# A mixture-of-experts step on one Trainium2 core: token lists of experts 19 to 63 read from a DRAM table instead of built by matmuls, with the weight loads in another order

## The chip, the cores and the metric

The kernel runs on one core of one Trainium2 chip. The metric is the device time of one execution in microseconds (us); for each kernel the median over several executions is given. The profile is of one execution, and its span runs from the first to the last instruction.

## The reference, cut to what matters

384 tokens (128 context, 256 latent) of width 1024 pass through one layer: attention and a convolution branch, then a mixture of experts, all in fp32. The change is in the mixture of experts:

```python
scores = jax.nn.sigmoid((t @ router_w).astype(jnp.float32))
...
_, idx = lax.top_k(masked, TOP_K)                      # 8 of 64 experts for each token
w = jnp.take_along_axis(scores, idx, axis=-1)
w = w / jnp.sum(w, axis=-1, keepdims=True) * ROUTED_SCALE
gates = jnp.sum(jax.nn.one_hot(idx, N_EXPERTS, dtype=jnp.float32) * w[..., None], axis=1)
hid = jax.nn.silu(jnp.einsum('td,edf->tef', t, exp_w_gate)) * jnp.einsum('td,edf->tef', t, exp_w_up)
hid = hid * gates[:, :, None].astype(hid.dtype)
routed = jnp.einsum('tef,efd->td', hid, exp_w_down)    # 64 experts, hidden width 256
shared = (jax.nn.silu(t @ sh_w_gate) * (t @ sh_w_up)) @ sh_w_down
return (routed + shared).reshape(B, S, D)
```

## The kernel before, in words

The first part (attention, convolution, router) ends near 510 us, and then a loop over the 64 experts runs. An expert takes one **step** j. Its tokens, 48 on average, are laid in 128 slots; if some expert had more than 128 tokens, the steps would go round again, and register `last` is read from the routing for that. With this input there is one round: 64 steps, in blocks of UNROLL = 8. `in_order` writes out block 0 with constant step numbers, runs a `Fori` loop over blocks 1 to 6, and writes out the last block.

Each fp32 product is made of three fp32r matmuls (high x high, high x low, low x high, lines 1759 to 1761). So ACT makes the high half of each weight tile (`gate_up_hi` L1072, `down_hi` L1081), and DVE the low half (`gate_up_lo` L1463, `down_lo` L1592). One step on each engine, in the order of its queue:

- SP: three loads of 1 MB into `raw`. Each tile has two buffers, and a load waits until DVE has made the low half from what was in the buffer: gate of expert j+3, then up of j+3 (both in `load_gate_up`, L636, semaphore `glo_done`), then down of j+1 (`load_down`, L643, `dlo_done`).
- POOL: `gather` (L777) fetches the rows of the tokens of j+3 from `h2_d` by the indices in `ixt`; `scatter` (L786) writes the results of j-3 to `y_d`.
- PE: `token_list` for j+3 (L2085), `turn_tokens` for j+1 (8 transposes, L1769), `gate_up` for j (24 matmuls of 512 columns), `turn_hidden` for j-1 (2 transposes), `down` for j-2 (12 matmuls of 512 columns).
- DVE: `hidden` (j-1), `hidden_lo` (j-2), `gate_up_lo` (j+1, gate), `list_of` (j+3, L1564 and L1565), `onehot` (j+4, L1552), `turn_lo` (j+1), `down_lo` (j-1), `gate_up_lo` (j+1, up).
- ACT: `gate_act`, `hidden_hi`, `gate_up_hi` (gate), `rows_out`, `turn_hi`, `down_hi`, `gate_up_hi` (up).

The token list of an expert comes about so: DVE compares each token's slot number with the 128 slots (`onehot`, 128x384), PE multiplies these three 128x128 matrices by four values of each token (`token_list`, three matmuls of 4 columns), and DVE copies the sums into `ixt` (row to gather, row to write) and `gsl` (the gate weight).

After the loop, the eight results of each token are read back from `y_d` (`first_rows` L663 to L667 on SP within the last block, the others after it), added up with the shared expert and the residual, and normed with `fgr`, the last norm's weights. `fgr` is loaded by ACT's queue just before the loop (L1165).

Of the kernel before, what the change touches and what calls it, by code (L numbers as in the profile page):

```python
# [26 lines left out]
P = 128  # L27
D = 1024
KD = D // P
NT = 3  # L30
# [18 lines left out]
UNROLL = 8  # L49
NO_TOKEN = 4096  # L50
TAIL_SUMS = 4 * NT + 4


def constants():

    import numpy as np

    i = np.arange(P)
    parts = {"ident": np.eye(P), "before": (i[:, None] < i[None, :]), "ones": np.ones((P, P)),
             "slot": np.broadcast_to((i % 8 * 16 + i // 8)[None, :], (P, P))}  # L60
# [11 lines left out]
    parts["token"] = i[:, None] + P * np.arange(NT)[None, :]  # L72
    at, n = {}, 0
# [65 lines left out]
def hybrid_step(nc, x_prompt, x_sample, cache_ckv, cache_krope, c, c_ctx, mod_w, mod_b, norm1_g, w_in,  # L139
# [11 lines left out]
    with ExitStack() as ctx:  # L151
# [124 lines left out]
        token_i = sb("token_i", [P, 1], A + 5.9375, I32)  # L276
        gsl = sb("gsl", [P, UNROLL], R + 8.375)
        sg = sb("sg", [P, FF], R + 9)
        hd = [sb(f"hd{i}", [P, FF], R + 10 + i) for i in range(2)]
# [20 lines left out]
        mod_d = dram("mod_d", [2, 4 * D])  # L300
        y_d = dram("y_d", [T * TOPK, D])

        def conv_slot(k):
# [17 lines left out]
        sinv = cst_of("sin").rearrange("p (t a f) -> p t a f", t=2, a=2)  # L321
        token = cst_of("token")
        V_G1, V_CB, V_LG, V_LB, V_QG, V_C = 0, 8, 16, 24, 32, 35

# [18 lines left out]
        cks_out = sem("cks_out")  # L343
        zeros_done, sgc_done, z_done, conv_step = (sem(n) for n in ("zeros_done", "sgc_done", "z_done", "conv_step"))
        sgs_done, sgs_out = sem("sgs_done"), [sem(f"sgs_out{i}") for i in range(2)]
        qtok_done, qrope_done, qT_act, qT_dve = (sem(n) for n in ("qtok_done", "qrope_done", "qT_act", "qT_dve"))
# [11 lines left out]
        x1_done, h2_done = sem("x1_done"), sem("h2_done")  # L358
        x1_out = sem("x1_out")
        h2d_out = sem("h2d_out")  # L360
        h2g_done, h2T_done = sem("h2g_done"), sem("h2T_done")
# [37 lines left out]
        def read_by(g):  # L399
# [6 lines left out]
                "lat": lambda: (lat_done, NT * n + g[2] + 1),  # L406
                "ca": lambda: (z_done, n + 1), "cg": lambda: (sgc_done, n + 1),
                "qnT": lambda: (f_done, KD + n + 1), "ckT": lambda: (flo_done, KD + 3 + n + 1),
                "krT": lambda: (krT_done, 1), "gl": lambda: (sgs_done, n + 1),
                "uq": lambda: (qtok_done, NT * n + g[2] + 1), "uk": lambda: (kT_done, 2 * n + 2),  # L410
# [132 lines left out]
        def _(sp):  # L543
# [183 lines left out]
        def _(pool):  # L727
            pool.memset(zb[:, :, :], 0.0).then_inc(zeros_done, 1)

            pool.wait_ge(latn_done, 2 * NT)  # L730
# [50 lines left out]
            def scatter(i, k, last=False):  # L781
# [26 lines left out]
        def _(act):  # L808
# [89 lines left out]
            for j in range(KD):  # L898
                split(item_no[("conv", j)] + 2)
                p = got(act, ("cg", j))  # L900
                if j >= 2:
                    act.wait_ge(z_done, j - 1)
                act.activation(sgc[:, j % 2, :], p[:, 0:T], ACT.Sigmoid).then_inc(sgc_done, 1)
                if j == 1:
# [9 lines left out]
            def spill_gate(j):  # L914

                act.wait_ge(sgs_done, j + 1)
                act.dma_start(sig_d[j], sgs[:, j % 2, :]).then_inc(sgs_out[j % 2], 16)


            for j in range(16):  # L920
# [3 lines left out]
                if j >= 2:  # L924
                    act.wait_ge(sgs_out[j % 2], 16 * (j // 2))
                act.activation(sgs[:, j % 2, :], p[:, 0:T], ACT.Sigmoid).then_inc(sgs_done, 1)
                if j:
# [188 lines left out]
            def step(i, k, left=99):  # L1116
# [68 lines left out]
        def _(dve):  # L1185
# [120 lines left out]
            for j in range(KD):  # L1306
                split(item_no[("conv", j)] + 2)
                g = ("ca", j)
                p = got(dve, g)
                dve.wait_ge(sgc_done, j + 1)  # L1310
                for a, b, o in ((0, TC, PAD), (TC, T, 2 * PAD + TC)):
# [243 lines left out]
            def list_of(i, k):  # L1555
                j = i * UNROLL + k
                if isinstance(j, int) and j < 2:
                    p = got(dve, ("list", j))
                else:
# [42 lines left out]
            def hidden(i, k):  # L1602
                j = i * UNROLL + k
                dve.wait_ge(sg_done, j + 1)
                if from_step(j, 2):
# [3 lines left out]
                                         op0=ALU.mult, op1=ALU.mult).then_inc(hd_done, 1)  # L1609

            sums = {"all": 0}

# [29 lines left out]
            def step(i, k, left=99):  # L1642
# [31 lines left out]
            turn_lo(0, 0)  # L1674
            shared_hidden(2)
            in_order(dve, step)


# [64 lines left out]
        def _(pe):  # L1743
# [521 lines left out]
```

## Time and profile before

| | |
|---|---|
| median of 3 executions | 1181.88 us (1179.66 to 1182.85) |
| the profiled execution | 1178.6 us |
| its span | 1176.8 us, mean granted clock 0.990 |
| PE busy | 1126.8 us, 96% of the span |
| DVE / ACT / POOL busy | 88% / 68% / 20% |
| read from and written to HBM | 326.66 MB and 41.66 MB |

A row of a group of instructions has its line, engine, operation, tiles (out<-in, buffer numbers left out), shapes and count, then the busy time in us and the mean ns of one, then the engine's idle time just before them and what ended it. Matmuls overlap: the duration of one is about 0.39 us, while the next starts 0.23 us after it. So a busy PE is read from the distance of the starts.

### The profile page before, as it was taken

What the parts mean: (1) busy time and instruction counts of PE and PEld (TensorE: products, weight loads), DVE (VectorE), ACT (ScalarE), POOL (GpSimd) and SP (SyncE); (2) the same over time, 40 slices, a digit from 0 to 9 for tenths busy, and PEclk for the clock granted to TensorE, in tenths of its full rate; (3) what the DMA queues carried; (4) which work ended last, traced back from release to release, by engine and by line L of the source; (5) the groups of instructions that cost most, each with busy time, mean ns of one, the idle gap of its engine ahead of it and who ended that gap; (6) DMA issues with size and microseconds to landing.
All of it is one profiled execution on the core that took longest, in us unless ns stands there. A gap on an engine that the chain in (4) does not pass through costs nothing.

```text
span 1176.8 us, 16800 instructions
## 1 busy us (share of the span) xinstructions
PE 1126.8 (96%) x5641; PEld 919.4 (78%) x5641; DVE 1031.0 (88%) x1379; ACT 801.6 (68%) x996; POOL 238.9 (20%) x184
## 2 busy tenths in 40 slices
PE   4999999998998999989999999999999999999996
PEld 1699999864557898658888888888888888888862
DVE  4759999989997465779999999999999999999977
ACT  6553232777873642648888888888888888888842
POOL 1000000001114001122533223332323323232220
PEclk9999999998999989999999999999999999999998
DMA  9673456535547236868999999999999999999994
GB/s 347 189 184 107 135 155 171 170 130 160 164 142 212 77 106 240 331 243 319 384 372 375 371 379 366 381 363 347 356 349 359 353 363 372 364 372 371 357 412 201
DMA packets 123035, 328.06 MB, mean 279 GB/s; under 512 B 28280, under 2 KB 69847, under 8 KB 98151
## 3 DMA queue, kind: packets, MB, share of 16 engines
q1 hardware_dynamic: 98368, 289.34, 67.1%
q0 software_dynamic: 21648, 33.80, 8.5%
q10 hardware_dynamic: 2968, 4.26, 1.0%
q8 instruction: 30, 0.49, 0.2%
q14 instruction: 21, 0.17, 0.0%
HBM read 326.66 MB, written 41.66 MB: 313 GB/s over the span
## 4 chain that ended last, share of the span: by engine, by line
PE 82%; DVE 6%; ACT 5%; DMA 5%; issue 2%; SPq 0%; POOLq 0%; ACTq 0%; DVEq 0%
PE bank L1759 22%; PE bank L1761 22%; PE bank L1760 21%; PE bank L1769 8%; PE bank L1954 2%; ACT hi L819 2%; PE bank L1942 2%; PE bank L2085 1%; DMA raw<-in_mod_w_dram 1%; DVE lo L1194 1%; DMA row3a<-y_d 1%; PE bank L1775 1%; PE bank L1776 1%; DMA xg<-h_d,ixt 1%; DMA raw<-in_exp_w_down_dram 1%
## 5 line engine op out<-in xcount | busy, mean ns | idle before, releaser
L1463 DVE TENSOR_TENSOR lgu<-raw,hgu 128x2048 fp32r<-128x2048 f32 x128 | 291.8, 2281 | 2.0 <-ACT hgu L1072 2.0
L1072 ACT ACTIVATE hgu<-raw 128x2048 fp32r<-128x2048 f32 x128 | 245.4, 1917 | 0.0
L1759 PE MATMUL bank<-hgu,xgh 128*128 128x512 f32 x512 | 205.9, 402 | 0.5 <-issue 0.3
L1761 PE MATMUL bank<-hgu,xgl 128*128 128x512 f32 x512 | 200.7, 392 | 0.0
L1760 PE MATMUL bank<-lgu,xgh 128*128 128x512 f32 x512 | 199.1, 389 | 0.0
L1592 DVE TENSOR_TENSOR lo<-raw,hi 128x2048 fp32r<-128x2048 f32 x64 | 147.7, 2308 | 25.5 <-ACT hi L1081 21.9
L1194 DVE TENSOR_TENSOR lo<-raw,hi 128x2048 fp32r<-128x2048 f32 (+2 forms) x57 | 125.5, 2205 | 29.8 <-ACT hi L819 29.8
L777 POOL DMA_INDIRECT xg<-h_d,ixt x64 | 66.2, 1034 | 392.6 <-DVE gsl L1565 362.3
L786 POOL DMA_INDIRECT y_d<-ys,ixt x62 | 127.8, 2061 | 48.4 <-ACT ys L1114 28.6
L1292 DVE SCALAR_TENSOR_TENSOR zb<-zb,cwt 128x400 f32<-128x400 f32 x240 | 135.5, 627 | 0.6
L1081 ACT ACTIVATE hi<-raw 128x2048 fp32r<-128x2048 f32 x64 | 122.8, 1919 | 8.4 <-DMA raw<-in_exp_w_down_dram 8.3
L819 ACT ACTIVATE hi<-raw 128x2048 fp32r<-128x2048 f32 (+2 forms) x57 | 105.1, 1846 | 18.9 <-PE bank L1761 16.0
L1761 PEld LDWEIGHTS bank<-hgu,xgl 128*128 128x128 f32 x512 | 96.1, 188 | 21.4
L1759 PEld LDWEIGHTS bank<-hgu,xgh 128*128 128x128 f32 x512 | 96.2, 188 | 19.2 <-DVE xgl L1598 1.1
L1760 PEld LDWEIGHTS bank<-lgu,xgh 128*128 128x128 f32 x512 | 96.4, 188 | 18.5
L1759 PE MATMUL bank<-hi,hdh 128*128 128x512 f32 x256 | 106.4, 416 | 0.3 <-DVE hdl L1639 0.3
L1761 PE MATMUL bank<-hi,hdl 128*128 128x512 f32 x256 | 100.7, 394 | 0.0
L1760 PE MATMUL bank<-lo,hdh 128*128 128x512 f32 x256 | 99.5, 389 | 0.0
L1759 PE MATMUL bank<-hTh,hi 128*128 128x384 f32 x256 | 85.6, 334 | 0.0
L1761 PE MATMUL bank<-hTh,lo 128*128 128x384 f32 x256 | 85.5, 334 | 0.0
L1760 PE MATMUL bank<-hTl,hi 128*128 128x384 f32 x256 | 85.5, 334 | 0.0
L1598 DVE TENSOR_TENSOR xgl<-bank,xgh 128x512 fp32r<-128x512 f32 x128 | 81.8, 678 | 1.8 <-ACT xgh L1089 1.8
(314 smaller groups left out, 2083.3 us busy)
## 6 DMA issues: line engine op xcount, KB each, us to landing
raw<-in_exp_w_gate_dram SPq DMA_DIRECT2D x64, 1024.0 KB
raw<-in_exp_w_up_dram SPq DMA_DIRECT2D x64, 1024.0 KB
raw<-in_exp_w_down_dram SPq DMA_DIRECT2D x64, 1024.0 KB
raw<-in_mod_w_dram SPq DMA_DIRECT2D x20, 1024.0 KB, 5.2
raw<-in_w_in_dram SPq DMA_DIRECT2D x16, 512.0 KB, 5.5
raw<-in_w_in_dram SPq DMA_DIRECT2D x8, 1024.0 KB, 5.3
mraw<-in_mod_w_dram SPq DMA_DIRECT2D x4, 1024.0 KB, 15.8
raw<-in_w_o_attn_dram SPq DMA_DIRECT2D x4, 1024.0 KB, 4.9
```

Of the source, the lines that this page charges most:

```text
L786: pool.indirect_dma_start(y_d, bass.IndirectOffsetOnAxis(ap=ixt[:, k % UNROLL, 1:2], axis=0), (ys_last if last else ys)[k % 2][:, :], None ...
L819: act.activation(hi[place(i)][:, 0:k * w], tile[:, 0:k * w], ACT.Copy).then_inc(hi_done, 1)
L1072: act.activation(hgu[k % 2][:, :, w, :], src, ACT.Copy).then_inc(ghi_done, 1)
L1081: act.activation(hi[down_place(k, last)][:, :], raw[s][:, :], ACT.Copy).then_inc(dhi_done, 1)
L1194: dve.tensor_tensor(lo[place(i)][:, 0:k * w], tile[:, 0:k * w], hi[place(i)][:, 0:k * w].bitcast(F32), ALU.subtract).then_inc(lo_done, 1)
L1292: ins = dve.scalar_tensor_tensor(out=dst, in0=src, scalar=wk, in1=dst, op0=ALU.mult, op1=ALU.add)
L1463: dve.tensor_tensor(lgu[k % 2][:, :, w, :], src, hgu[k % 2][:, :, w, :].bitcast(F32), ALU.subtract).then_inc(glo_done, 1)
L1592: dve.tensor_tensor(lo[to][:, :], raw[s][:, :], hi[to][:, :].bitcast(F32), ALU.subtract).then_inc(dlo_done, 1)
L1759: pe.matmul(out, ah, bh, start=first, stop=False)
L1760: pe.matmul(out, ah, bl, start=False, stop=False)
L1761: return pe.matmul(out, al, bh, start=False, stop=last)
L1769: return pe.transpose(out, src, ident[0:n, 0:n])
```

## The change

It has five parts.

1. **Entries.** DVE computes once, before the loop (`entry_rows`, 17 small operations), where each of a token's eight choices belongs: a row of a new DRAM table `lists_d` with 64 x 3 lists of 128 slots, 4 words a row. In steps 2 to 13 it computes two gate weights per step (`entry_gates`, 24 operations of 64 columns, each with a sum as its second output).
2. **Table.** POOL fills `lists_d` at the very start with a value that no index has (393 KB, in runs of 512 bytes), writes 24 x 128 entries of 16 bytes into it by indirect DMA (`write_lists`, two DMAs in each of steps 2 to 13), and in step 14 loads the table back into `listed` (393 KB).
3. **Lists.** Up to expert 18 the lists are made as before. From expert 19 on (ON_TENSOR = 19), `list_of` copies two indices and a gate weight from `listed`; `onehot` and `token_list` are gone. That is 45 experts, in steps 16 to 60. `in_order` writes out two blocks (BLOCKS = 2), and the loop begins at block 2.
4. **Loads.** In a step SP issues gate of j+3, down of j+1, up of j+3.
5. **fgr.** Its load moves from before the loop to the last block, behind the last list, since `listed` lies in the same memory.

Two pairs of semaphores are also made one (`sig_done`), and the constants grow by 88 columns (45 KB). The core of the diff:

```diff
+KEY = 2048
+BLOCKS = 2
+ON_TENSOR = BLOCKS * UNROLL + 3
+FIRST_SENT = 2
...
-            for k in range(UNROLL):
-                step(0, k)
-            with eng.Fori(1, last) as i:
+            for i in range(BLOCKS):
+                for k in range(UNROLL):
+                    step(i, k)
+            with eng.Fori(BLOCKS, last) as i:
...
                 if left > 3:
-                    load_gate_up(i, k + 3)
+                    load_gate_up(i, k + 3, parts=(0,))
                 if left == 2:
                     first_rows(i)
                 if left > 1:
                     load_down(i, k + 1)
+                if left > 3:
+                    load_gate_up(i, k + 3, parts=(1,))
...
+            pool.wait_ge(con_in, 16)
+            pool.dma_start(lists_d.rearrange("(q a) v -> q (a v)", q=P).rearrange("q (b n) -> q b n", n=P),
+                           ones.unsqueeze(1).to_broadcast([P, NJ * 4 // P, P])).then_inc(lists_out, 16)
...
+            def write_lists(first):
+
+                for n in (first, first + 1):
+                    t, u = n // TOPK, n % TOPK
+                    pool.wait_ge(entry_done, n + 1)
+                    pool.indirect_dma_start(lists_d, bass.IndirectOffsetOnAxis(ap=entry_row[:, t, u:u + 1], axis=0),
+                                            entry[:, t, u, :], None,
+                                            bounds_check=P * NJ - 1, oob_is_err=False).then_inc(lists_out, 16)
...
+                if isinstance(j, int) and FIRST_SENT <= j < FIRST_SENT + 12:
+                    write_lists(2 * (j - FIRST_SENT))
+                if isinstance(j, int) and j == FIRST_SENT + 12:
+                    pool.wait_ge(lists_out, 16 * (NT * TOPK + 1))
+                    pool.dma_start(listed[:, :, :], lists_d.rearrange("(q j) v -> q j v", q=P)).then_inc(lists_out, 16)
...
+                if left == 3:
+                    listed_all = value(act, i * UNROLL + UNROLL)
+                    act.wait_ge(rtab_done, 1)
+                    act.wait_ge(list_done, listed_all)
+                    act.dma_start(fgr[:, :], final_g.rearrange("(a n) -> a n", a=1).partition_broadcast(P)).then_inc(tail_in, 16)
...
-            act.wait_ge(x1_out, 48)
-            act.dma_start(fgr[:, :], final_g.rearrange("(a n) -> a n", a=1).partition_broadcast(P)).then_inc(tail_in, 16)
...
+                if not isinstance(j, int) or j >= ON_TENSOR:
+                    dve.wait_ge(lists_out, 16 * (NT * TOPK + 2))
+                    dve.tensor_copy(ixt[:, k % UNROLL, :], listed[:, bass.ds(j, 1), 0:2].rearrange("p a v -> p (a v)").bitcast(I32))
+                    dve.tensor_copy(gsl[:, k % UNROLL:k % UNROLL + 1],
+                                    listed[:, bass.ds(j, 1), 2:3].rearrange("p a v -> p (a v)")).then_inc(list_done, 1)
+                    return
...
+            def entry_gates(first):
+
+                for n in (first, first + 1):
+                    t, u = n // TOPK, n % TOPK
+                    if n >= 8:
+                        dve.wait_ge(entry_done, n - 7)
+                    dve.scalar_tensor_tensor(out=key_gate[:, n % 8, :], in0=keys[:, t, :], scalar=key8[:, t, u:u + 1],
+                                             in1=gates[:, t, :], op0=ALU.is_equal, op1=ALU.mult,
+                                             accum_out=entry[:, t, u, 2:3]).then_inc(entry_done, 1)
...
-                if left > 4:
+                if isinstance(j, int) and j + 4 < ON_TENSOR:
                     onehot(i, k + 4)
                 if left > 1:
                     turn_lo(i, k + 1)
+                if isinstance(j, int) and FIRST_SENT <= j < FIRST_SENT + 12:
+                    entry_gates(2 * (j - FIRST_SENT))
...
+            entry_rows()
             in_order(dve, step)
...
-                if left > 3:
+                if isinstance(j, int) and j + 3 < ON_TENSOR:
                     token_list(i, k + 3)
```

PE in the loop, from the last matmul of `down` (hi, hdl) to the transposes of the gathered rows (con, xg), before:

```order
L1761 MATMUL bank<-hi_154,hdl_181 128x512
L2076 REGISTER_ALU
L2085 ISA [waits list_done,oh_done]
L2085 MATMUL bank<-vals,oh_171 128x4
L2085 ISA
L2085 MATMUL bank<-vals,oh_171 128x4
L2085 ISA
L2085 MATMUL bank<-vals,oh_171 128x4
L2114 REGISTER_ALU [waits gathered1]
L1769 MATMUL bank<-con,xg_163 128x128 [waits xgl_done]
L1769 MATMUL bank<-con,xg_163 128x128 x7
L2121 REGISTER_ALU
```

and now, with the first matmul of `gate_up` as well:

```order
L1847 MATMUL bank<-hi_154,hdl_192 128x512
L2200 ISA [waits gathered1]
L1855 MATMUL bank<-con,xg_163 128x128 [waits xgl_done]
L1855 MATMUL bank<-con,xg_163 128x128 x7
L2207 REGISTER_ALU
L1845 MATMUL bank<-hgu_158,xgh_164 128x512 [waits glo_done,hd_done,xgl_done]
```

The three matmuls with their register instructions and their wait for `oh_done` and `list_done` are gone; the transposes stand right behind `down`.

SP in block 0, three loads of one step and of the next, before:

```order
L636 DMA raw_49<-in_exp_w_gate_dram 128x2048 [waits glo_done]
L636 DMA raw_50<-in_exp_w_up_dram 128x2048 [waits glo_done]
L643 DMA raw_51<-in_exp_w_down_dram 128x2048 [waits dlo_done]
L636 DMA raw_52<-in_exp_w_gate_dram 128x2048 [waits glo_done]
L636 DMA raw_150<-in_exp_w_up_dram 128x2048 [waits glo_done]
L643 DMA raw_151<-in_exp_w_down_dram 128x2048 [waits dlo_done]
```

and now:

```order
L655 DMA raw_49<-in_exp_w_gate_dram 128x2048 [waits glo_done]
L662 DMA raw_51<-in_exp_w_down_dram 128x2048 [waits dlo_done]
L655 DMA raw_50<-in_exp_w_up_dram 128x2048 [waits glo_done]
L655 DMA raw_52<-in_exp_w_gate_dram 128x2048 [waits glo_done]
L662 DMA raw_151<-in_exp_w_down_dram 128x2048 [waits dlo_done]
L655 DMA raw_150<-in_exp_w_up_dram 128x2048 [waits glo_done]
```

The down load (`raw_51`, `raw_151`) has moved ahead of the up load, and its wait (`dlo_done`) now stands ahead of the up load's (`glo_done`).

DVE in step 2, from the list to the end of the step (`lo_157` is the down tile's low half, `lgu_161` that of up), now:

```order
L1722 TENSOR_TENSOR hdl_191<-bank,hdh_189 128x256 [waits hdh_done]
L1504 TENSOR_TENSOR lgu_161<-raw_52,hgu_159 128x8x256 [waits ghi_done]
L1611 TENSOR_SCALAR ixt<-bank 128x2 [waits list_filled]
L1612 TENSOR_REDUCE gsl<-bank 128x1
L1593 TENSOR_TENSOR oh_170<-con,pos_129 128x384 [waits list_filled]
L1645 TENSOR_TENSOR xgl_167<-bank,xgh_165 128x512 [waits xgh_done] x2
L1690 SCALAR_TENSOR_TENSOR key_gate,entry<-keys,key_181,gates 128x64 x2
L1639 TENSOR_TENSOR lo_157<-raw_151,hi_154 128x2048 [waits dhi_done]
L1504 TENSOR_TENSOR lgu_161<-raw_150,hgu_159 128x8x256 [waits ghi_done]
```

The two gate weights stand between `turn_lo` and `down_lo`, whose wait is for ACT (`dhi_done`). POOL in steps 2 to 4, now:

```order
L801 DMA xg_163<-h_d,ixt 128x1024 [waits xt_filled,list_done,rtab_done]
L820 DMA lists_d<-entry,entry_row 24576x4 [waits entry_done] x2
L801 DMA xg_162<-h_d,ixt 128x1024 [waits xt_filled,list_done,rtab_done]
L810 DMA y_d<-ys_168,ixt 3072x1024 [waits ys_done,rtab_done]
L820 DMA lists_d<-entry,entry_row 24576x4 [waits entry_done] x2
L801 DMA xg_163<-h_d,ixt 128x1024 [waits xt_filled,list_done,rtab_done]
L810 DMA y_d<-ys_169,ixt 3072x1024 [waits ys_done,rtab_done]
```

Two list writes follow the gather (step 2) and each gather and scatter after it; before, gathers and scatters stood alone.

## Rows read from the trace of the kernel before

**Rows 1.** The page, part 1: busy us (share of the span) xinstructions.

```profile
PE 1126.8 (96%) x5641; PEld 919.4 (78%) x5641; DVE 1031.0 (88%) x1379; ACT 801.6 (68%) x996; POOL 238.9 (20%) x184
```

**Rows 2.** Windows; busy (x) of PE, PEld, DVE, ACT, POOL, PEclk, DMA, GB/s.

```profile
0.00:36.00 36.00, 18.80 (x79) 7.88 (x80) 19.55 (x15) 24.47 (x26) 3.89 (x5) 1.00 0.99 353
560.00:600.00 40.00, 40.00 (x204) 33.84 (x204) 38.91 (x42) 33.77 (x39) 19.93 (x9) 1.00 0.97 383
600.00:1100.00 500.00, 500.00 (x2537) 423.02 (x2536) 477.16 (x519) 427.96 (x466) 151.75 (x104) 1.00 0.95 365
1120.00:1150.00 30.00, 29.66 (x109) 19.34 (x107) 23.16 (x22) 11.04 (x17) 6.32 (x6) 1.00 1.03 414
```

**Rows 3.** Timeline of PE in three steps; columns: start us, us, engine line op.

```profile
1094.72 0.39 PE L1761 MATMUL bank<-hi,hdl 128*128 128x512 f32 x1
1094.95 0.39 PE L2085 MATMUL bank<-vals,oh 128*128 x3
1095.20 1.09 PE L1769 MATMUL bank<-con,xg 128*128 128x128 f32 x8
1096.05 0.47 PE L1759 MATMUL bank<-hgu,xgh 128*128 128x512 f32 x1
...
1104.39 0.39 PE L1761 MATMUL bank<-hi,hdl 128*128 128x512 f32 x1
1104.62 1.03 PE L1769 MATMUL bank<-con,xg 128*128 128x128 f32 x8
1105.41 0.48 PE L1759 MATMUL bank<-hgu,xgh 128*128 128x512 f32 x1
...
1113.98 1.03 PE L1769 MATMUL bank<-con,xg 128*128 128x128 f32 x8
```

**Rows 4.** Groups by line, 600 to 1100 us; columns as in the page's part 5.

```profile
L1463 DVE TENSOR_TENSOR lgu<-raw,hgu 128x2048 fp32r<-128x2048 f32 x104 | 237.2, 2281 | 0.0
L1592 DVE TENSOR_TENSOR lo<-raw,hi 128x2048 fp32r<-128x2048 f32 x52 | 120.2, 2312 | 22.8 <-ACT hi L1081 19.2 <-issue 3.5
L1081 ACT ACTIVATE hi<-raw 128x2048 fp32r<-128x2048 f32 x52 | 99.7, 1918 | 4.4 <-DMA raw<-in_exp_w_down_dram 4.4
L786 POOL DMA_INDIRECT y_d<-ys,ixt x52 | 101.5, 1952 | 17.9 <-issue 17.9
L1552 DVE TENSOR_TENSOR oh<-con,pos 128x384 fp32r<-128x384 f32 x51 | 27.8, 545 | 0.0
```

**Rows 5.** DMA view, 600 to 1100 us.

```profile
DMA packets 37305, 182.49 MB, mean 365 GB/s; under 512 B 12642, under 2 KB 12642, under 8 KB 17438
```

**Rows 6.** Timeline, SP's queue and ACT: a down load and its reader.

```profile
804.60 0.38 SPq L643 DMA_DIRECT2D raw<-in_exp_w_down_dram  x1
...
816.97 1.92 ACT L1081 ACTIVATE hi<-raw 128x2048 fp32r<-128x2048 f32 x1
```

**Rows 7.** Timeline of the loop's start.

```profile
515.59 0.99 POOL L777 DMA_INDIRECT xg<-h_d,ixt  x1 [2.53 <-PE bank L1769]
516.49 0.34 ACTq L1165 DMA_DIRECT2D fgr<-in_final_g_dram  x1
520.04 0.16 DVE L1564 TENSOR_SCALAR ixt<-bank 128x2 int32<-128x2 f32 x1 [2.64 <-PE bank L2085]
527.24 1.09 PE L1769 MATMUL bank<-con,xg 128*128 128x128 f32 x8 [3.05 <-DMA xg<-h_d,ixt]
```

**Rows 8.** Chain that ended last, first piece; columns: start us, us, what.

```profile
2.30 14.02 DMA raw<-in_mod_w_dram
```

**Rows 9.** DMA view, 300 to 450 us: packets, MB, share of 16.

```profile
q0 software_dynamic: 832, 0.05, 2.4%
```

**Rows 10.** A 64-column DVE group, and an accumulator read on ACT (timeline).

```profile
L1510 DVE MAX8 rk<-rsel 128x8 f32<-128x64 f32 x3 | 0.5, 215 | 0.0
...
14.89 0.18 ACT L855 ACTIVATION_READ_ACCUMULATOR junk<-x 128x1 f32 x1
```

**Rows 11.** Chain of work that ended last, at the last down load.

```profile
1120.39 8.15 DMA raw<-in_exp_w_down_dram
```

More of the change, by code:

```diff
@@ L72, in constants @@
     parts["token"] = i[:, None] + P * np.arange(NT)[None, :]
+    parts["key"] = np.broadcast_to(KEY * (NE - np.arange(NE))[None, :], (P, NE))
+    parts["dest"] = (TOPK * parts["token"][:, :, None] + np.arange(TOPK)).reshape(P, NT * TOPK)
     at, n = {}, 0
@@ L277, in hybrid_step @@
         gsl = sb("gsl", [P, UNROLL], R + 8.375)
+        listed = sb("listed", [P, NJ, 4], A + 105)
+        entry = sb("entry", [P, NT, TOPK, 4], A + 7.25)
+        entry_row = sb("entry_row", [P, NT, TOPK], A + 7.625, I32)
+        keys = sb("keys", [P, NT, NE], A + 105)
+        gates = sb("gates", [P, NT, NE], A + 105.75)
+        key_gate = sb("key_gate", [P, 8, NE], A + 106.5)
+        key8 = sb("key8", [P, NT, TOPK], A + 108.5)
+        key_i, key_p, key_q, key_r = (sb(f"key_{n}", [P, NT, TOPK], R + 15.125 + 0.125 * i, I32)
+                                      for i, n in enumerate("ipqr"))
         sg = sb("sg", [P, FF], R + 9)
@@ L301, in hybrid_step @@
         y_d = dram("y_d", [T * TOPK, D])
+        lists_d = dram("lists_d", [P * NJ, 4])
         def conv_slot(k):
@@ L322, in hybrid_step @@
         token = cst_of("token")
+        key_of, dest = cst_of("key"), cst_of("dest").rearrange("p (t s) -> p t s", t=NT)
         V_G1, V_CB, V_LG, V_LB, V_QG, V_C = 0, 8, 16, 24, 32, 35
@@ L343, in hybrid_step @@
         cks_out = sem("cks_out")
-        zeros_done, sgc_done, z_done, conv_step = (sem(n) for n in ("zeros_done", "sgc_done", "z_done", "conv_step"))
-        sgs_done, sgs_out = sem("sgs_done"), [sem(f"sgs_out{i}") for i in range(2)]
+        zeros_done, sig_done, z_done, conv_step = (sem(n) for n in ("zeros_done", "sig_done", "z_done", "conv_step"))
+        sgs_out = [sem(f"sgs_out{i}") for i in range(2)]
         qtok_done, qrope_done, qT_act, qT_dve = (sem(n) for n in ("qtok_done", "qrope_done", "qT_act", "qT_dve"))
@@ L359, in hybrid_step @@
         x1_out = sem("x1_out")
+        entry_done, lists_out = sem("entry_done"), sem("lists_out")
         h2d_out = sem("h2d_out")
@@ L406, in read_by @@
                 "lat": lambda: (lat_done, NT * n + g[2] + 1),
-                "ca": lambda: (z_done, n + 1), "cg": lambda: (sgc_done, n + 1),
+                "ca": lambda: (z_done, n + 1), "cg": lambda: (sig_done, n + 1),
                 "qnT": lambda: (f_done, KD + n + 1), "ckT": lambda: (flo_done, KD + 3 + n + 1),
-                "krT": lambda: (krT_done, 1), "gl": lambda: (sgs_done, n + 1),
+                "krT": lambda: (krT_done, 1), "gl": lambda: (sig_done, KD + n + 1),
                 "uq": lambda: (qtok_done, NT * n + g[2] + 1), "uk": lambda: (kT_done, 2 * n + 2),
@@ L902, in _ @@
                     act.wait_ge(z_done, j - 1)
-                act.activation(sgc[:, j % 2, :], p[:, 0:T], ACT.Sigmoid).then_inc(sgc_done, 1)
+                act.activation(sgc[:, j % 2, :], p[:, 0:T], ACT.Sigmoid).then_inc(sig_done, 1)
                 if j == 1:
@@ L914, in spill_gate @@
             def spill_gate(j):
-                act.wait_ge(sgs_done, j + 1)
+                act.wait_ge(sig_done, KD + j + 1)
                 act.dma_start(sig_d[j], sgs[:, j % 2, :]).then_inc(sgs_out[j % 2], 16)
@@ L925, in _ @@
                     act.wait_ge(sgs_out[j % 2], 16 * (j // 2))
-                act.activation(sgs[:, j % 2, :], p[:, 0:T], ACT.Sigmoid).then_inc(sgs_done, 1)
+                act.activation(sgs[:, j % 2, :], p[:, 0:T], ACT.Sigmoid).then_inc(sig_done, 1)
                 if j:
@@ L1309, in _ @@
                 p = got(dve, g)
-                dve.wait_ge(sgc_done, j + 1)
+                dve.wait_ge(sig_done, j + 1)
                 for a, b, o in ((0, TC, PAD), (TC, T, 2 * PAD + TC)):
@@ L1558, in list_of @@
                     p = got(dve, ("list", j))
-                else:
+                elif isinstance(j, int) and j < ON_TENSOR:
                     dve.wait_ge(list_filled, j - 1)
@@ L1609, in hidden, with entry_rows @@
                                          op0=ALU.mult, op1=ALU.mult).then_inc(hd_done, 1)
+            def entry_rows():
+                first = pos3[:, :, 0:NE]
+                dve.wait_ge(x1_out, 48)
+                dve.tensor_tensor(gates[:, :, :], vals[:, :, 2, :].bitcast(F32), vals[:, :, 3, :].bitcast(F32), ALU.add)
+                link(dve, "v", dve.scalar_tensor_tensor(out=keys[:, :, :], in0=first, scalar=512.0,
+                                                        in1=key_of.unsqueeze(1).to_broadcast([P, NT, NE]),
+                                                        op0=ALU.is_lt, op1=ALU.mult))
+                link(dve, "v", dve.tensor_tensor(keys[:, :, :], keys[:, :, :], first, ALU.add))
+                for t in range(NT):
+                    ins = dve.max(key8[:, t, :], keys[:, t, :])
+                dve.tensor_copy(entry[:, :, :, 0].bitcast(I32), token.unsqueeze(2).to_broadcast([P, NT, TOPK]))
+                for v in (1, 3):
+                    dve.tensor_copy(entry[:, :, :, v].bitcast(I32), dest)
+                link(dve, "v", ins)
+                link(dve, "v", dve.tensor_copy(key_i[:, :, :], key8[:, :, :]))
+                dve.tensor_scalar(key_p[:, :, :], key_i[:, :, :], 7, 4, ALU.bitwise_and, ALU.logical_shift_left)
+                dve.tensor_scalar(key_r[:, :, :], key_i[:, :, :], 1, NE * 3, ALU.logical_shift_right, ALU.bitwise_and)
+                link(dve, "v", dve.tensor_scalar(key_q[:, :, :], key_i[:, :, :], 3, 15, ALU.logical_shift_right, ALU.bitwise_and))
+                link(dve, "v", dve.tensor_tensor(key_p[:, :, :], key_p[:, :, :], key_q[:, :, :], ALU.add))
+                dve.tensor_scalar(key_q[:, :, :], key_i[:, :, :], 11, None, ALU.logical_shift_right)
+                link(dve, "v", dve.scalar_tensor_tensor(out=key_p[:, :, :], in0=key_p[:, :, :], scalar=float(NJ),
+                                                        in1=key_r[:, :, :], op0=ALU.mult, op1=ALU.add))
+                link(dve, "v", dve.scalar_tensor_tensor(out=entry_row[:, :, :], in0=key_p[:, :, :], scalar=float(NE),
+                                                        in1=key_q[:, :, :], op0=ALU.add, op1=ALU.subtract))
```

## The prediction

> **What bounds the kernel now.** I read the page first: PE is busy 96% of the span, DVE 88% [rows 1]. A share over the whole span doesn't say what a change in one stage is worth, so the windows come next. In the 500 us of the loop's middle PE has no idle time at all, at full granted clock, while DVE has 477 of 500 us, ACT 428, POOL 152, and the DMA engines 0.95 [rows 2]. Then PE's timeline, since a busy PE can hide slack: from the last matmul of `down` in one step to that in the next it is 1104.39 - 1094.72 = 9.67 us, and each matmul starts as soon as the one before lets it [rows 3]. The loop runs at PE's pace: what leaves PE's queue there shortens each step, until the next resource is reached. The next ones are near. DVE stands idle 22.8 us in 52 steps, 0.44 us a step, waiting for ACT's high half of the down tile [rows 4]. The DMA engines move 182.49 MB in 500 us, 3.53 MB a step [rows 5], which takes them 0.95 x 9.67 = 9.19 us of the step.
>
> **What the lists take from PE.** The last block holds the experiment already. Step 60 has a `token_list`, steps 61 and 62 have none. With it, from the last `down` matmul to the first of `gate_up` is 1096.05 - 1094.72 = 1.33 us; without, 1105.41 - 1104.39 = 1.02 us. That is 0.31 us, of which 0.25 lie ahead of the transposes (1095.20 against 1104.62) and the rest within them. The whole step agrees: the transposes of steps 61 and 62 start 1113.98 - 1104.62 = 9.36 us apart [rows 3]. 45 steps without a list: 45 x 0.31 = **14.0 us saved**; 11.3 if only the 0.25 counts. In the same steps DVE loses a `onehot` of 545 ns [rows 4], and two small copies stand where two small operations stood, so DVE is no obstacle there.
>
> **DVE's new work.** `entry_rows` is 17 small operations before the loop, some 0.2 us each by the 215 ns of a 64-column one [rows 10], 3.4 us. DVE then stands idle 2.64 us for the list matmul of step 0, and PE later waits 3.05 us for a gather [rows 7]; the 0.8 us left over lies ahead of that wait. I cost it at nothing; without the cover it would be 3.4. `entry_gates` adds two operations to each of steps 2 to 13. No row shows one on DVE. The low bound is 0.215 us, a 64-column operation; the high one adds an accumulator read like ACT's 0.18, 0.395 us [rows 10]. I take 0.3, so 0.6 us a step against 0.44 us of idle time that stands at just this place, ahead of `down_lo`: 0.16 x 12 = **1.9 us lost** (0 to 0.35 x 12 = 4.2), since at the start of the loop PE has no lead over DVE to spend.
>
> **fgr.** Its 0.52 MB were asked for at 516.49, just when the gather issued at 515.59 was under way that PE waited for until 527.24 [rows 7]. At 383 GB/s [rows 2] they are 1.4 us. PE could start that much sooner, but DVE's chain follows close; I take half, **0.7 us gained**. Now they are loaded in the last block, ahead of a stretch in which the DMA engines are full (share 1.03 at 414 GB/s) [rows 2], and the chain goes through the last down load for 8.15 us [rows 11]. Up to 1.3 us, of which part falls into gaps, and 0.4 for a queue that is fuller after faster steps: **1.2 us lost** (0 to 1.7).
>
> **The fill of the table.** 0.39 MB, with 0.05 MB more constants, meet the first 36 us, where the DMA share is 0.99 at 353 GB/s [rows 2], and the chain begins with 14.02 us of a weight load [rows 8]. 0.44 / 353 = **1.2 us lost**. Nothing hides it if that load is behind it (0), and if short runs cost what small packets cost (next part) it is 768 x 69 ns / 16 = 3.3 us.
>
> **The list writes.** 256 entries of 16 bytes in each of 12 steps. The nearest row is that of many small writes from the same queue: 832 packets took 2.4% of 16 engines for 150 us, 69 ns each [rows 9]. 256 x 69 ns / 16 = 1.1 us a step, on top of 9.19: 0.6 us over the step, 7.5 us in 12 steps. PE doesn't feel that at once, since loads come early: a down load has 816.97 - 804.60 = 12.4 us [rows 6], three loads of 1 MB take 8.2 at 383 GB/s, the new order adds 2.3, so some 6.5 us are a cushion; ACT waited for a load only 4.4 us in 52 steps [rows 4]. That leaves **1.0 us lost**. The bounds are nothing and, at the mean of all packets in the loop (0.95 x 500 x 16 us / 37305 = 204 ns [rows 2, 5]), 3.3 us a step, 27 us in all after the cushion. POOL has room: its scatter takes 1952 ns [rows 4], two more like it give some 7 us of a step. The table's reload is 1 us of DMA once, issued two steps ahead of its first reader.
>
> The Trainium skill ("DMA: Bandwidth & Descriptors", Measured) gives small packets a floor of about 10.5 ns each, while below 512 bytes a write is read, changed and written back (Specifications). By the first figure the writes would be an estimated 0.2 us a step and cost nothing; the rows above show 69 ns, and I go by them.
>
> **The order of the loads.** It moves the down load ahead of the up load on SP, past its wait. DVE makes the low half of down first, so the down load goes out some 2.3 us (one 2281 ns operation [rows 4]) sooner, with 14.7 us instead of 12.4 before its reader; up follows as it did, but behind 1 MB more. The order is then that in which ACT reads. PE never waited for a load in the middle of the loop, so by itself this is worth 0; it is cover for shorter steps. In step 1 alone `down_lo` stands behind the up half, and the up load goes out 2 us later, with 12 us in hand. One more block written out costs nothing on any engine.
>
> **Sum.** -14.0 + 1.9 - 0.7 + 1.2 + 1.2 + 1.0 = **-9.4 us**. The profiled execution took 1178.6 us, its span 1176.8; it would be 1169.2. The median of the runs is 1181.88, 3.3 us above that execution, so on the median I predict 1172.5 us.
>
> **Rivals.**
>
> 1. *The DMA engines become the bound.* 3.53 MB in 9.36 us is 377 GB/s and a share of 0.98. For it: the down loads that came late. Against: 383 GB/s for 40 us and 414 for 30 [rows 2]. If the step ends at 9.50, the gain is 45 x 0.17 = 7.7 instead of 14.0: -3.1 us, 1178.8.
> 2. *They are the bound already, and no list saving shows.* Then all that is added counts: -9.4 + 14.0 = 4.6 us slower, 1186.5. Against it: PE is idle nowhere, and steps 61 and 62 did shorten, to 9.36 [rows 3]. The Trainium skill (same page, Specifications) names some 358 GB/s as a core's share of the memory, which for 3.53 MB would be an estimated 9.86 us a step. The trace doesn't agree: 365 on average, 414 for 30 us; the page itself gives more to a core whose neighbour rests.
> 3. *DVE leads in steps 2 to 13.* Gates at 0.395 us make DVE's step 9.67 + 0.35: 4.2 us lost instead of 1.9, 1174.8.
> 4. *The small writes are dear.* They share the engines with weight loads that have half a microsecond to spare a step. Without the 1.0 I counted, 10.4 us of gain are left; with x us a packet the loss is 12 x (16x - 0.48) - 6.5, which eats them from x = 0.12 on. Some way to the other bound, at 150 ns, it is 16.5: 1188, slower. For it: share 0.95 leaves no room. Against: 69 ns in the only row of its kind.
>
> **How the numbers follow.** The forecast has 0.63, rival 1 0.14, rival 2 0.03, rival 3 0.12, rival 4 0.08. The forecast's own range: 14.0 with everything added at its low bound and the gain of fgr gives 1167; with the upper bounds of gates, fill and tail it is 1177.4. Rival 3 lies within that, rival 1 mostly below 1180. So 1167 to 1180 leaves out rivals 2 and 4 and the rest of the first, less than 2 in 10. 0.3% is 3.5 us, about what a measurement of this kernel tells from no change. Faster by more than that: 0.63 + 0.12 + a third of rival 1, 0.79. Within it: the rest of rival 1 and a mild case of rival 4, 0.11. Slower: 0.10.
>
> **What would show it.** PE's steps from 16 on 9.36 us apart, before that 9.67; PE without waits there; no `vals` matmuls past expert 18. DVE's wait for ACT ahead of `down_lo` near nothing in steps 2 to 13 and longer after. ACT's waits for the down load gone or fewer. The first mod_w load about 1 us later; the wait for the first gathers about 1 us shorter. I am wrong if PE waits for `lgu` in steps 2 to 13, if ACT waits for `raw` in each step, if DVE stands at the first list from the table, or if a list write takes POOL over 3 us.

## The result, and the profile after

| | before | after |
|---|---|---|
| median of the runs, us | 1180.93 (1179.66 to 1182.85, 4 runs) | 1210.45 (1207.09 to 1214.79, 4 runs) |
| ratio, 95% interval | | 1.0251 (1.0232 to 1.0271) |
| span of the profiled execution, us | 1176.8 | 1209.9 |

The change made the kernel 2.5% slower. The forecast was 1172.5 us, 1167 to 1180, with 0.79 on faster. It is wrong in its sign, and the measured time lies 30 us above the range.

Of the page of the kernel after: busy time by engine, shares of the chain that ended last, and the three groups whose waits grew. Columns are as in the page of before; the last is the idle time ahead of the group and what ended it.

```profile
PE 1130.2 (93%) x5506; PEld 909.6 (75%) x5506; DVE 1019.3 (84%) x1399; ACT 798.6 (66%) x996; POOL 319.1 (26%) x210
...
PE 46%; DMA 32%; DVE 11%; ACT 8%; issue 3%; POOL 0%; SPq 0%; POOLq 0%; DVEq 0%; ACTq 0%
...
L1504 DVE TENSOR_TENSOR lgu<-raw,hgu 128x2048 fp32r<-128x2048 f32 x128 | 292.4, 2285 | 52.5 <-ACT hgu L1110 52.5
L1110 ACT ACTIVATE hgu<-raw 128x2048 fp32r<-128x2048 f32 x128 | 245.4, 1917 | 77.4 <-DMA raw<-in_exp_w_up_dram 65.8
L1845 PE MATMUL bank<-hgu,xgh 128*128 128x512 f32 x512 | 206.2, 403 | 26.1 <-DVE lgu L1504 25.2
```

Before, PE had no wait in the middle of the loop [rows 2, 3]. Now ACT waits 65.8 us for the up load, DVE waits for ACT, and PE for DVE. The chain in the loop (start us, us, what) is load, `hgu`, `lgu`, load, some 20 us for two steps:

```profile
899.97 1.93 ACT hgu L1110
...
901.92 2.30 DVE lgu L1504
...
904.24 14.99 DMA raw<-in_exp_w_up_dram
...
919.26 1.93 ACT hgu L1110
...
921.21 2.30 DVE lgu L1504
...
923.53 15.71 DMA raw<-in_exp_w_up_dram
```

The windows (columns as in [rows 2]) of the kernel after:

```profile
560.00:600.00 40.00, 40.00 (x204) 33.79 (x203) 39.84 (x63) 34.34 (x38) 34.69 (x17) 1.00 0.97 369
600.00:1100.00 500.00, 479.72 (x2328) 395.68 (x2327) 444.90 (x477) 410.04 (x450) 203.65 (x113) 1.00 0.97 354
```

The DMA share rose from 0.95 to 0.97 while the rate fell from 365 to 354 GB/s. PE's clock was full, so the clock is no cause here.

ACT's `sg` comes once a step, so it marks the steps. In the timeline of ACT, steps 18 and 61 of before:

```profile
695.82 0.39 ACT L1097 ACTIVATE sg<-bank 128x256 f32<-128x256 f32 x1 [0.47 <-PE bank L1761]
...
1111.16 0.39 ACT L1097 ACTIVATE sg<-bank 128x256 f32<-128x256 f32 x1 [0.67 <-PE bank L1761]
```

and steps 3, 18, 61 and 63 of after:

```profile
554.11 0.39 ACT L1135 ACTIVATE sg<-bank 128x256 f32<-128x256 f32 x1 [4.44 <-PE bank L1847]
...
698.15 0.39 ACT L1135 ACTIVATE sg<-bank 128x256 f32<-128x256 f32 x1 [0.57 <-PE bank L1847]
...
1134.94 0.36 ACT L1135 ACTIVATE sg<-bank 128x256 f32<-128x256 f32 x1
...
1159.77 0.37 ACT L1135 ACTIVATE sg<-bank 128x256 f32<-128x256 f32 x1
```

The 43 steps from 18 to 61 took 415.34 us before, 9.66 each, and 436.79 after, 10.16 each. That is 21.5 of the 33.1 us between the spans, where I had expected 13 us less. The last two steps add 5.6 (24.83 against 19.22), the stretch behind them 3.7, the first three steps 1.2, the start of the loop 2.1; steps 3 to 18 took 1.0 less. Steps 3 to 14 are 9.67 as before. Steps 16 and 17, the first with lists from the table, took 9.35, as forecast. From step 18 on loads come late (ACT's first wait for one is at 706.10 us), so the trouble begins with the rows that the table's lists place.

Reading `entry_rows` again gave a suspect. The lists of before put position s of an expert at partition (s mod 16) x 8 + s div 16. The table puts it at (s mod 8) x 16 + s div 8. Both stand in the kernels' code, the second in `entry_rows`, whose lines are left out of the diff above; I had counted the operations of `entry_rows` and not worked out where they send a token. With 48 tokens, 3 lie in each block of 8 partitions before, and 6 or 0 in the table's.

### The profile page after: what moved, and what is told of

Same layout as the page of the kernel before. It is cut to its first block, busy times and chain, and to the rows that moved or that the text cites. A ratio compares the mean times of both kernels' runs of the same rounds, so it can differ in the third digit from the quotient of the medians.

```text
span 1209.9 us, 16277 instructions
## 1 busy us (share of the span) xinstructions
PE 1130.2 (93%) x5506; PEld 909.6 (75%) x5506; DVE 1019.3 (84%) x1399; ACT 798.6 (66%) x996; POOL 319.1 (26%) x210
## 4 chain that ended last, share of the span: by engine, by line
PE 46%; DMA 32%; DVE 11%; ACT 8%; issue 3%; POOL 0%; SPq 0%; POOLq 0%; DVEq 0%; ACTq 0%
DMA raw<-in_exp_w_up_dram 25%; PE bank L1845 11%; PE bank L1847 11%; PE bank L1846 11%; DVE lgu L1504 5%; PE bank L1855 3%; ACT hgu L1110 3%; DMA raw<-in_exp_w_gate_dram 3%; PE bank L2040 2%; ACT hi L857 2%; PE bank L2028 1%; PE bank L1861 1%; DMA raw<-in_mod_w_dram 1%; PE bank L1862 1%; DMA raw<-in_exp_w_down_dram 1%
## 5 line engine op out<-in xcount | busy, mean ns | idle before, releaser
L1110 ACT ACTIVATE hgu<-raw 128x2048 fp32r<-128x2048 f32 x128 | 245.4, 1917 | 77.4 <-DMA raw<-in_exp_w_up_dram 65.8
L810 POOL DMA_INDIRECT y_d<-ys,ixt x62 | 150.9, 2433 | 53.5 <-issue 26.9
```

The lines of the kernel that those rows point to most:

```text
L810: pool.indirect_dma_start(y_d, bass.IndirectOffsetOnAxis(ap=ixt[:, k % UNROLL, 1:2], axis=0), (ys_last if last else ys)[k % 2][:, :], None ...
L1110: act.activation(hgu[k % 2][:, :, w, :], src, ACT.Copy).then_inc(ghi_done, 1)
```

## The experiments

Four theories. **T1**: the placement loads some DMA engines more than others. **T2**: the new order of loads. **T3**: the DMA engines' limit, which shorter steps reach. **T4**: something else in how lists come from the table. Unless said otherwise, times are medians, and intervals are of the ratio to the kernel before.

**Put the placement back in the changed kernel (e1), or put it into the kernel before (e2).**

```
e1: key_p = (key & 15) << 3     was (key & 7) << 4
    key_q = (key >> 4) & 7      was (key >> 3) & 15
e2: "slot": i % 16 * 8 + i // 16     was i % 8 * 16 + i // 8
```

> The changed kernel, with one thing put back: the 48 tokens of an expert lie in the table where the lists of before put them (three to each block of 8 partitions), not six to every other block. T1 (placement: the gathers and scatters of six-and-none load some DMA engines twice as much as others): the steps from 16 on fall from 10.2 us to PE's 9.36 to 9.5, ACT's waits for raw (66 us for up, 16 for down) mostly go, the time is 1168 to 1180. T2 (order of the loads) and T3 (the DMA engines' limit, which faster steps reach) and T4 (something in the table's way of making lists): it stays at 1205 to 1212, steps at 10.2.

> The kernel before, with one constant changed: its matmul lists put tokens where the table puts them (six to every other block of 8 partitions), in all 64 experts. Nothing else moves. T1: all steps of the loop go to 10.0 to 10.3 us, 60 steps by 0.5, so 1205 to 1217. T2, T3, T4: no difference, 1180 to 1183.

e1: 1171.91 us, 0.9922 (0.9900 to 0.9945). e2: 1212.96 us, 1.0272 (1.0249 to 1.0296). Taking the placement away from the changed kernel removes the loss, and adding it alone to the kernel before makes the loss. So the placement is its cause. T1's numbers came, those of the others did not. The windows of e1, then of e2:

```profile
600.00:1100.00 500.00, 498.91 (x2461) 417.51 (x2460) 468.96 (x503) 432.49 (x479) 223.11 (x120) 1.00 0.99 376
```

```profile
600.00:1100.00 500.00, 487.91 (x2436) 406.94 (x2435) 456.46 (x495) 398.27 (x449) 117.16 (x98) 1.00 0.91 350
```

e2 has the share 0.91, less than the 0.95 of before, and is bound by its loads: ACT's `hi` (groups by line, 600 to 1100 us) waited 100.1 us for the down load, against 4.4 before [rows 4].

```profile
L1081 ACT ACTIVATE hi<-raw 128x2048 fp32r<-128x2048 f32 x49 | 94.0, 1919 | 100.1 <-DMA raw<-in_exp_w_down_dram 100.1
```

**The order of the loads, back to gate, up, down in e1 (e3), and new in the kernel before (e4).**

```
e3:  load_gate_up(i, k + 3)      was parts=(0,), with parts=(1,) behind load_down
e4:  the reverse, in the kernel before
```

> As e1_a_spread, and the loads in the order gate, up, down of before. T1: like e1_a_spread within 3 us (1168 to 1182). T2: the order costs, so this one alone comes to about 1170 while e1_a_spread stays near 1210. T3, T4: both near 1210.

> The kernel before with the new order of loads (gate, down, up) alone. T1, T3, T4: 1179 to 1184, PE's steps 9.67, since PE never waited for a load. T2: 1195 or more, with ACT waiting for the up load in each step.

e4: 1181.40 us, 0.9999 (0.9987 to 1.0010), no difference, as expected. e3: 1181.80 us, 1.0001 (0.9987 to 1.0015), and that no theory had foreseen: T1 wanted it within 3 us of e1, and T2 wanted e3 the faster. With the placement of before, the changed kernel is no faster than the kernel before in the old order, and 10 us faster in the new one. The saving wasn't all gone: in the profiled execution of e3 (1179.5 us, the fastest of its ten) steps 18 to 61 took 406.5 us, 8.8 less than before and 3.5 more than in e1. ACT's wait for loads in e3, and in e1 (groups by line, 600 to 1100 us):

```profile
L1117 ACT ACTIVATE hi<-raw 128x2048 fp32r<-128x2048 f32 x53 | 102.1, 1927 | 42.5 <-DMA raw<-in_exp_w_down_dram 42.2
```

```profile
L1110 ACT ACTIVATE hgu<-raw 128x2048 fp32r<-128x2048 f32 x107 | 205.9, 1924 | 18.2 <-DMA raw<-in_exp_w_up_dram 14.9 <-DMA raw<-in_exp_w_gate_dram 3.2
```

So the placement of before also stands near a limit. Which partitions belong together was the next question.

**Two more placements in the kernel before (e5, e6).**

```
e5:  "slot": i//4%8 + 8*(i//64) + 16*(i%4) + 64*(i//32%2)
e6:  "slot": i
```

> The kernel before with a third placement in its matmul lists. Placement matters (e1_a_spread, e2_b_packed), and this run tells which partitions go together. If the 16 groups are blocks of 8 consecutive partitions (M1), this placement is uneven in the same way as the table's: the tokens lie six to each of 8 blocks, none in the other 8, so it comes to about 1213 like e2_b_packed. If a group is 4 partitions and the 4 that stand 32 further on (M2, the Trainium skill's rule for a transfer to 128 partitions, DMA Engines, The descriptor swizzle), this placement is the even one, three to each group, and the one of before was the uneven one: 1181 or less, the DMA share falling below 0.95.

(The page's title is "DMA: Bandwidth & Descriptors".)

> The kernel before with the tokens of an expert in consecutive partitions from 0 on, the most uneven placement. By M1 the busiest group has 8 rows in and 8 out a step (196.6 KB of weights and 8 x 8.2 KB, 262 KB, against 221 with three rows and 246 with six); at the 24 KB a us that 221 KB in 9.19 us make, the step becomes 10.9 us and the time 1181 + 60 x 1.2 = about 1255 (1240 to 1265). By M2 the busiest group has 8 here and 8 in e2_b_packed, so the time is that of e2_b_packed, 1208 to 1218. If it is not placement by groups but something of the table's pattern alone, 1181.

e5: 1180.31 us, 0.9992 (0.9975 to 1.0010). e6: 1193.43 us, 1.0114 (1.0091 to 1.0137). M1, blocks of 8 partitions in a row, wanted 1213 and 1255, and falls with both. It was how I had first thought of T1. But M2 didn't foresee these numbers either: it wanted e6 equal to e2, 20 us higher, and the DMA share of e5 to fall below 0.95, where it is 0.96.

Both expectations had taken 48 tokens for every expert. The numbers that the reference's routing gives for this input run from 8 to 118. Counted with them, M2's fullest group holds on average 3.5 rows in e5, 6.1 in the placement of before, 6.8 in e6 and 7.6 in e2. That is the measured order. A 4096-byte packet of a gather or scatter took 164 ns on average in the kernel before, between 700 and 1100 us; this mean is from the trace's packet records and stands in no view shown here. A row is two such packets, so the differences from 6.1 make 0.22 and 0.47 us a step, 13 and 28 us in 60 steps; measured are 13 and 31. The counting came after these runs, so it is a fit, and needed a test. Its order says more than its size: the sum takes 9.67 us for the limit at 6.1 rows, but e3 ran that placement, in the same old order, at 9.45 us a step (18 to 61), and from there 0.47 gives 9.92 for e2, which took 10.11.

**A placement made by M2, with the new order, the old order, and in the kernel before (e9, e10, e11).**

```
"slot": i % 4 * 32 + i // 4
e9, e10 also:  key_p = (key & 31) << 2,  key_q = (key >> 5) & 3
```

> The changed kernel with a fourth placement for matmul lists and table alike: position s of a list goes to partition (s mod 32) x 4 + s div 32. M2 (groups of 4 partitions and the 4 that stand 32 further on) explained the first four: counted with the numbers of tokens that this input gives the experts, its fullest group has 6.1 rows on average in the placement of before, 3.5 in e5_b_v, 6.8 in e6_b_ident, 7.6 in e2_b_packed, and at 2 x 164 ns a row the differences from 6.1 are 0.22 and 0.47 us a step, for 13 and 29 us measured as 13 and 31. Here the fullest group has 3.7. M2: the DMA engines no longer set any step, so this is as fast as e1_a_spread or faster, 1166 to 1172. M3 (groups by partition bits 0, 1, 3, 6, the only other choice of four bits that puts the four placements in the measured order): the fullest group has 7.9 rows, 1215 or more.

> e9_a_r2 with the loads in the order gate, up, down. With the placement of before that order took the whole gain (e3_a_spread_old 1182 against 1172). If it did so because the fullest DMA engines stood just at the limit (M2: 6.1 rows), the even placement frees it: 1168 to 1174, within 3 us of e9_a_r2. If the old order costs by itself in steps of 9.36 us (the down load goes out too late), it stays near 1180.

> The kernel before with the placement of e9_a_r2 alone. M2: PE sets the step, 1178 to 1182, no difference. M3: 1220 or more.

e9: 1169.27 us, 0.9913 (0.9887 to 0.9940). e10: 1169.61 us, 0.9904 (0.9878 to 0.9929). e11: 1180.15 us, 0.9996 (0.9980 to 1.0012). All three are M2's, and M3 (groups by partition bits 0, 1, 3 and 6) is excluded. e10 also explains e3: with an even placement the old order costs nothing, so its 10 us hang on the placement, as they would if the fullest group stood near its limit. Windows of e9, and its steps 18 and 61:

```profile
600.00:1100.00 500.00, 500.00 (x2470) 419.06 (x2469) 470.25 (x507) 433.71 (x479) 232.55 (x120) 1.00 0.99 377
```

```profile
699.30 0.39 ACT L1135 ACTIVATE sg<-bank 128x256 f32<-128x256 f32 x1 [0.67 <-PE bank L1847]
...
1101.49 0.39 ACT L1135 ACTIVATE sg<-bank 128x256 f32<-128x256 f32 x1 [0.68 <-PE bank L1847]
```

402.19 us for 43 steps, 9.35 each, with PE never idle from 600 to 1100 us. e9 and e10 beat the kernel before by about 1%, and the changed one by more. Against e1 (9.37 a step) their intervals overlap, so they are not proven faster than it.

**Does the uneven load pile up, or does each transfer delay by itself (e12)?**

```
e2, with  slot[:, k % 2 * 8 : k % 2 * 8 + P]    (a constant 8 longer)
```

> e2_b_packed with the placement turned by 8 partitions in every odd step, so that the groups that hold 8 rows in one step (M2) hold none or few in the next. The fullest group of a single step has 7.6 rows as before; over two steps it is 4.7 a step. If what counts is the work that piles up on one DMA engine over more than a step, since loads come a step ahead, this is as the kernel before, 1179 to 1184. If each single gather or scatter with 8 rows on an engine delays the loads behind it, it stays at 1205 to 1213.

1184.80 us, 1.0025 (1.0009 to 1.0040). Of the 31 us that e2 lost, 1 to 5 remain, and its steps 18 to 61 take the 415.34 us of before. So the load piles up over steps: a group that is full in one step and nearly empty in the next costs almost nothing.

**What the table costs without its use (e7), and the old order in the slow kernel (e8).** e7 is e1 with every list made by matmul; the table is filled, written and loaded, and nothing is copied from it.

```
e7:  elif isinstance(j, int) and j < ON_TENSOR:   ->  else:
     if j + 4 < ON_TENSOR: onehot                 ->  if left > 4: onehot
     if j + 3 < ON_TENSOR: token_list             ->  if left > 3: token_list
e8:  the changed kernel with load_gate_up(i, k + 3)
```

> e1_a_spread with all lists made by matmul as before; the table is filled, written and loaded, but no list is copied from it. What the table's making costs then stands alone. My sum: fill 1.2, gates 1.9, list writes 1.0, fgr -0.7 and 1.2: 4.6 us over before, 1186. If the cover is larger than I took it to be (e1_a_spread came within 1 us of my forecast, but with the order of loads in it, which I had priced at nothing), it is 1181 to 1183; if the list writes are dear, over 1190.

> The changed kernel, its table's placement kept, with the loads in the order gate, up, down of before. In the spread placement the new order was worth 10 us (e3_a_spread_old against e1_a_spread). If the order works by keeping the queue of loads fuller, it does so in the packed case too: 1215 to 1222. If it only covers shorter steps that PE could make, it is worth nothing where the DMA engines set the step: 1208 to 1212.

e7: 1185.70 us, 1.0072 (1.0043 to 1.0101). The medians differ by 5.5 us, the interval says 5 to 12, so my 4.6 is at its low edge or below. Its steps 18 to 61 took 415.34 us, 9.66 each, against 9.35 in e9. e8: 1213.81 us, 1.0292 (1.0245 to 1.0338); that overlaps with the changed kernel and both of the expected cases, so it decides nothing.

## Why the prediction was wrong, point by point

- **What failed** is no term of the sum but one that is missing, and so put at nothing without a reason: what the table's placement of tokens does to the DMA engines. "`entry_rows` is 17 small operations before the loop" costed the time of these operations and not their result. The placement of tokens in partitions is part of the change, and it costs the kernel before 31 us when nothing else is changed (e2). With the old placement back, the changed kernel takes 1171.9 us (e1), where I had forecast 1172.5. That agreement is in part luck: it needs the new order of the loads, which I had priced at nothing (without it 1181.8, e3), and several terms were off.
- **Lists off PE, 14.0 us saved**: right. 9.66 a step with lists (e7), 9.35 without (e9), 0.31 as read from the last block [rows 3]. In the changed kernel it showed in steps 16 and 17 alone, and from then on loads set the step.
- **The order of the loads, 0**: right at steps of 9.67 us (e4) and with an even placement (e9, e10), and 10 us short with the placement of before (e1 against e3). I had called it "cover for shorter steps" and then priced that cover at nothing. Had the order been left out, the forecast would have missed by 10 us even with the old placement.
- **`entry_gates`, 1.9 us over 12 steps**: the size is near by luck, and the way was another. A gate takes 274 ns and its accumulator read 78, partly beside each other, so that two gates take 0.41 us (groups by line, 541 to 663 us, of after):

```profile
L820 POOL DMA_INDIRECT lists_d<-entry,entry_row x24 | 53.8, 2241 | 7.9 <-issue 7.0 <-DVE key_gate L1690 0.9
...
L1690 DVE SCALAR_TENSOR_TENSOR key_gate<-keys,key,gates 128x64 f32<-128x64 f32 x24 | 5.7, 274 | 0.0
L1690 DVE DVE_READ_ACCUMULATOR key_gate<-keys,key,gates 128x1 f32 x24 | 1.9, 78 | 0.0
```

  Steps 3 to 14 stay at 9.67, so the gates cost nothing there, and rival 3 with its loss in each step is out. A loss shows in step 2 alone, where PE waited for `lgu`, one of my signs of being wrong: 13.3 to 13.4 us in the seven kernels with the table, 10.0 to 11.3 in the seven without. The nearest of these are e4 and e5, whose first two steps took 14.4 to 14.7 us, like those of the kernels with the table. There PE waited 1.21 and 1.46 us in this place and kept its clock, and the first three steps took 25.7; with the table it waited 1.82 to 1.86 and its clock fell, and they took 27.7. Of these 2.0 us some 0.4 to 0.6 are the longer wait, which fits the two gates ahead of it, and the rest is the clock (last section). The other five without the table took longer over the first two steps, and 25.8 to 28.1 for the three. No run leaves the gates out, so that the longer wait is theirs is argued.
- **List writes, 1.0 us, and rival 4**: mis-sized, and rival 4 is out. I had counted 256 packets a step at 69 ns. The trace's packet records (they stand in no view shown here) have 384 packets of 128 bytes from POOL's queue between 547 and 661 us, and none in the kernel before: 32 a step, of 15 ns on average, 0.03 us of all 16 engines in place of 1.1. The 832 packets of [rows 9] were half of 4 bytes at 8 ns and half of 128 bytes at 133, so their mean of 69 was that of neither. POOL took 2241 ns for a write, under the 3 us that I had named. Steps 3 to 14 show no price either, but for 0.7 us in e3, which e8, with the same gathers and loads up to there, doesn't have.
- **Fill, 1.2 us**: some 0.4. The first load of the chain ends its wait after 14.26 us, against 14.02 [rows 8]; it is 14.15 to 14.76 in the seven kernels with the table and 13.69 to 14.02 in the seven without. In the packet records the fill is 96 packets of 4096 bytes at 170 ns, 1.0 us of all engines, so the short runs that I feared (768 packets) don't show.

```profile
2.30 14.26 DMA raw<-in_mod_w_dram
```

- **fgr, -0.7 and +1.2**: not told apart. The start of the loop lies between 524.3 and 528.4 us in kernels that don't differ there (before, e4, e5, e11), which is more than the 0.7. At the end of the changed kernel ACT waited 9 us for the last down load (below), but there the loads were late anyway. In the kernels with the table whose loop no load held up (e7, e9, e10), steps 61 to 63 took 19.7 to 20.3 us, against 18.3 to 19.4 in the like ones without (before, e4, e5, e11, e12). That is about 1 us, as priced, but no run moves `fgr` alone.
- **Rival 1**, the DMA engines become the bound, came true in kind, though for the fullest ones: in e3 for a good part of the gain, in e1 for a little (9.37 a step against the 9.35 of e9). I had looked for it in the mean share and the mean rate, and had worked out the cushion of 6.5 us from the mean too. The mean was no guide: 0.91 in e2, which is bound by loads, 0.99 in e9, which isn't. **Rival 2** is out, since the saving shows where the placement is even. The 358 GB/s that the Trainium skill gives as a core's part ("DMA: Bandwidth & Descriptors", Specifications) don't bind this kernel: e9 moved 377 for 500 us.

## What to carry to other kernels

When a change writes indices, work out where they send the data, with real counts, before pricing the instructions that make them. A mean DMA share near 1 doesn't say whether the engines are the bound, and one of 0.91 doesn't say that they aren't: look for who waits for a load. Spread the valid rows of a gather or scatter over the partition groups, or turn the placement from step to step.

## What the runs showed of the hardware that was not expected

**Partitions and DMA engines.** Five placements in the kernel before, and three in the changed one, agree with groups made of 4 partitions and the 4 that stand 32 further on. The Trainium skill states this for a plain transfer to 128 partitions ("DMA: Bandwidth & Descriptors", The descriptor swizzle), as the partitions that one engine serves; here indirect gathers and scatters behave so. M1 and M3 are excluded. Of all groupings by some of the seven partition bits, counted with the routing of this input, one other puts the placements in the measured order, two such groups taken together (bits 2, 3, 6); it gives 12.1 rows to the placement of before and 12.4 to e6, whose times are 13 us apart, so it fits badly. Groupings that mix bits in other ways were not tried, and the trace shows no engine by itself, so that the full thing is an engine is inferred.

The sizes don't come out either. Taken at its word, M2 gives the fullest engine the mean time (share x step) and 0.33 us for each row above the mean of 3: an estimated 9.2 + 1.0 = 10.2 us a step in the kernel before, which took 9.67 and didn't wait, and 9.2 + 1.5 = 10.7 in e2, which took 10.11. Packet times can overlap, since shares above 1 occur [rows 2]. So the count ranks placements and doesn't give the step's time; what sets it in full stays open.

**A short wait, and PE at half clock.** In step 2 of the changed kernel PE waited 1.82 us for `lgu`, and then its matmuls started 0.43 us apart and no longer 0.23 (timeline of PE):

```profile
546.78 0.47 PE L1845 MATMUL bank<-hgu,xgh 128*128 128x512 f32 x1 [1.82 <-DVE lgu L1504]
...
547.31 0.59 PE L1847 MATMUL bank<-hgu,xgl 128*128 128x512 f32 x1
547.70 0.63 PE L1845 MATMUL bank<-hgu,xgh 128*128 128x512 f32 x1
548.12 0.63 PE L1846 MATMUL bank<-lgu,xgh 128*128 128x512 f32 x1
...
550.96 0.39 PE L1847 MATMUL bank<-hgu,xgl 128*128 128x512 f32 x1
```

Windows of the changed kernel there, and behind its last down load; the granted clock is the third number from the end, and 0.50 is 1.2 GHz:

```profile
548.00:554.00 6.00, 6.00 (x22) 4.78 (x22) 6.00 (x12) 1.67 (x1) 3.15 (x2) 0.77 0.97 372
...
1161.00:1165.20 4.20, 4.07 (x11) 3.32 (x12) 4.20 (x4) 0.77 (x2) 1.48 (x1) 0.50 1.03 415
```

In the same place e11 waited 0.17 us and kept its clock:

```profile
546.13 0.47 PE L1759 MATMUL bank<-hgu,xgh 128*128 128x512 f32 x1 [0.17 <-DVE lgu L1463]
```

```profile
548.00:554.00 6.00, 6.00 (x29) 4.96 (x28) 6.00 (x8) 4.83 (x5) 3.83 (x2) 1.00 0.97 404
```

From 547.31 to 550.96 nine matmuls started in 3.65 us, where at 0.23 they take 2.1: the fall cost 1.6 us. The other six kernels with the table have the same fall behind waits of 1.83 to 1.86 us (in windows of 6 us around it the clock is 0.72 to 0.86). e4 and e5, with waits of 1.21 and 1.46 us in this place, kept 1.00. At the end of the changed kernel the fall follows this wait of ACT, behind which PE stood idle for 4.86 us:

```profile
1157.96 1.91 ACT L1119 ACTIVATE hi<-raw 128x2048 fp32r<-128x2048 f32 x1 [9.00 <-DMA raw<-in_exp_w_down_dram]
```

That the idle time brought the clock down is read from the order of these events and from the kernels side by side; no run changed the wait alone.
